# A two-layer network in float32 on one core: eight block products replaced by seven in the input, output and gate projections

## What is computed

```python
h = rmsnorm(x, norm_mix_g)
u = h @ w_in                                     # 2048 x 12288
c_g, b_g, xa, za, q, fl, iv, og, ga, gb = jnp.split(u, split_idx, axis=-1)
ya = b_g * causal_dwconv3(c_g * xa, conv_w) * silu(za)
o = hgrn2_chunked(silu(q), kk(fl), iv, log_f(fl))          # 8 heads of 128
yb = headnorm(o) * hg_norm_g * silu(og)
m = sigmoid(ga) * (ya @ w_a_out) + sigmoid(gb) * (yb @ w_b_out)
x = x + m @ w_o                                  # 2048 x 2048
gate = sigmoid(rmsnorm(x, ple_norm_g) @ w_ple_gate)        # 2048 x 2048
x = x + gate * (p @ w_ple_proj)
x = rmsnorm(x, final_norm_g)
mod = silu(c_2) @ w_ada_2 + b_ada_2              # 2048 x 6144, one row
shift, scale, gate2 = jnp.split(mod, 3)
proj = (rms_norm(x, norm_gain_2) * (1 + scale) + shift) @ w_in_2   # 2048 x 7168
out = (attention and retention of proj, gated) @ w_out_2   # 2048 x 2048
return rms_norm(x + gate2 * out, final_gain_2)
```

## Time and profile before

| | |
|---|---|
| median of 3 runs | 2703.95 us (2701.43 to 2704.10) |
| the profiled execution | 2703.86 us |
| its span in the profile | 2702.6 us |
| TensorE, busy share of the span | 98% |
| VectorE | 47% |
| ScalarE | 33% |
| GpSimd | 4% |
| mean granted clock of TensorE | 0.991 of full speed |

### The profile page before, as it was taken

The page is one execution under the profiler, slowest core; times in us unless marked ns, Lnnn a source line. Parts: engine busy times, 40 slices in busy tenths (PEclk is TensorE's granted clock), DMA queues, the critical chain, the costliest instruction groups (busy, mean ns, idle before and its releaser), DMA issues.

```text
span 2702.6 us, 28694 instructions
## 1 busy us (share of the span) xinstructions
PE 2641.6 (98%) x11724; PEld 2135.7 (79%) x11724; DVE 1267.1 (47%) x1782; ACT 879.9 (33%) x1218; POOL 98.7 (4%) x79
## 2 busy tenths in 40 slices
PE   8999999999999999999999999999999999998996
PEld 6888888888888888888888888688767777776885
DVE  7546634457334555655433444552333444442433
ACT  5533324333222222222222433332232333342331
POOL 3000000000000000000001012000000000000011
PEclk9999999999999999999999999999999999998998
DMA  5322233222334666666442222244222222221422
GB/s 179 100 79 76 76 90 101 85 71 72 90 97 141 207 206 202 202 207 206 135 161 94 86 101 86 71 146 131 75 70 78 75 81 71 78 72 53 172 94 78
DMA packets 155075, 303.86 MB, mean 112 GB/s; under 512 B 10752, under 2 KB 11008, under 8 KB 153920
## 3 DMA queue, kind: packets, MB, share of 16 engines
q1 hardware_dynamic: 154144, 300.46, 34.8%
q0 software_dynamic: 224, 1.15, 0.1%
q10 hardware_dynamic: 576, 0.43, 0.0%
HBM read 293.60 MB, written 8.39 MB: 112 GB/s over the span
## 4 chain that ended last, share of the span: by engine, by line
PE 92%; DVE 4%; issue 2%; ACT 1%; DMA 0%; POOL 0%; SPq 0%; DVEq 0%; ACTq 0%; POOLq 0%
PE bank L327 83%; PE bank L667 2%; PE bank L1099 1%; PE bank L1203 1%; PE bank L1177 1%; PE bank L383 1%; DVE WL L359 1%; PE bank L686 1%; DVE XL L452 1%; PE bank L1192 1%; PE bank L1088 1%; PE bank L324 0%; PE bank L322 0%; DMA X<-in_xT 0%; PE bank L954 0%
## 5 line engine op out<-in xcount | busy, mean ns | idle before, releaser
L327 PE MATMUL bank<-XH,WH 128*128 128x512 f32 x2816 | 1143.1, 406 | 17.3 <-DVE XL L452 10.4
L327 PE MATMUL bank<-XH,WL 128*128 128x512 f32 x2816 | 1105.8, 393 | 17.9 <-DVE WL L359 17.9
L327 PE MATMUL bank<-XL,WH 128*128 128x512 f32 x2816 | 1101.6, 391 | 0.0
L359 DVE TENSOR_TENSOR WL<-RAW,WH 128x1024 fp32r<-128x1024 f32 x436 | 538.2, 1236 | 956.5 <-ACT WH L345 955.7
L345 ACT CAST WH<-RAW 128x1024 fp32r<-128x1024 f32 x436 | 455.9, 1048 | 1209.9 <-PE bank L327 1204.5
L327 PEld LDWEIGHTS bank<-XH,WH 128*128 128x128 f32 x2816 | 533.0, 189 | 140.9 <-issue 31.4
L327 PEld LDWEIGHTS bank<-XH,WL 128*128 128x128 f32 x2816 | 531.8, 189 | 135.8 <-DVE WL L359 21.3
L327 PEld LDWEIGHTS bank<-XL,WH 128*128 128x128 f32 x2816 | 532.9, 189 | 122.9 <-issue 15.8
L327 PE MATMUL bank<-WH,XH 128*128 128x512 f32 x384 | 154.2, 401 | 0.0
L327 PE MATMUL bank<-WL,XH 128*128 128x512 f32 x384 | 149.6, 390 | 0.0
L327 PE MATMUL bank<-WH,XL 128*128 128x512 f32 x384 | 149.4, 389 | 0.0
(11 more groups left out here) (247 smaller groups left out, 1688.3 us busy)
## 6 DMA issues: line engine op xcount, KB each, us to landing
RAW<-in_w_in SPq DMA_DIRECT2D x304, 512.0 KB, 3.6
AST<-in_w_ada SPq DMA_DIRECT2D x192, 256.0 KB, 3.8
RAW<-in_w_o SPq DMA_DIRECT2D x32, 512.0 KB, 3.6
RAW<-in_w_gate SPq DMA_DIRECT2D x32, 512.0 KB, 3.6
RAW<-in_w_out SPq DMA_DIRECT2D x32, 512.0 KB, 3.6
RAW<-in_w_a SPq DMA_DIRECT2D x16, 512.0 KB, 4.1
RAW<-in_w_b SPq DMA_DIRECT2D x16, 512.0 KB, 4.3
XT<-in_xT SPq DMA_DIRECT2D x4, 1024.0 KB, 6.7
```

Of the source, the lines that this page charges most:

```text
L327: ins = nc.tensor.matmul(bank[b][:, :], l, r, start=first, stop=final)
L359: nc.vector.tensor_tensor(WL[:, m % NSPL], RAW[:, m % NRAW], WH[:, m % NSPL].bitcast(F32), ALU.subtract).then_inc(lo.sem, lo.step(m))
```

## The change

For `w_in` (all but the first 16 units), `w_o` and `w_gate`, each product of a 2x2 arrangement of blocks is made with seven products instead of eight: the 2048 features are two halves (tile k and tile k + 8), the output columns are two halves (c1 and c2), the sequence is two halves of 256 rows. The seven right-hand sides are sums of the four activation blocks, made once per operand (`sums_pool` on GpSimd, `combine_act`, `combine_dve`); the seven left-hand sides are sums of the four weight blocks, made per unit on VectorE (`weight_sums`). The seven results lie in seven halves of four banks and are added up by `seven_first` (ScalarE) and `seven_out` (VectorE). A unit is now 128 rows twice by two blocks, 256 KB, four blocks of 128 x 128; there are 872 units, of which 496 have seven products. The host lays the weights out in the order of use, and no arithmetic is done there. The other products (`raw`, `wa`, `wb`, `proj`, the second block) keep their three times four matmuls of 512 columns per unit.

The order goes by head pairs p and p + 4: `fl, q, iv, cg, xa, bg, za, og` for one pair after the other (a group is 8 units of 256 columns of output). The first 16 units make `fl` and `q` of pair 0 from the undivided x. `ga` 0 to 2 come early, the rest of `ga` and all `gb` after the pairs, `wa` and `wb` then. Branches (`y_dram`), sigmoids of the gates (`g_dram`) and `proj` (`p_dram`) go to DRAM and come back. The last third of the sum over `w_ada` moves into the second block.

```diff
+    def seven(*groups, n=8):
+        for k in range(n):
+            for name, w, c1, c2 in groups:
+                r1, r2 = 128 * k, 128 * (k + n)
+                UNITS.append((w, [(r1, c2), (r1, c1), (r2, c2), (r2, c1)]))
...
+SEVEN_PRODUCTS = ((1, 0, 1, 4), (1, 1, 4, 3), (2, 0, 3, 6), (2, 1, 6, 1), (0, 0, 2, 2), (0, 1, 5, 5), (3, 0, 0, 0))
+def split_upto(n):
+    return min(n + 2 if n else 0, len(UNITS) - 1) + 1
+def sums_upto(n):
+    return min(n + 3, len(UNITS) - 1) + 1
+def load_upto(n):
+    return min(split_upto(n) + NRAW, len(UNITS))
...
+    def pe_seven(names, ready):
...
+                for j in range(3):
...
+                    for r, half, x, wt in SEVEN_PRODUCTS:
+                        first = k == 0 and j == 0 and half == 0 and not (u and r == 3)
+                        if first and gone[u, r]:
+                            T.wait_ge(gone[u, r][0], (yield gone[u, r]))
+                        h = half or (u if r == 3 else 0)
+                        wo = (WL if j == 2 else WH)[:, s, wt]
+                        ins = nc.tensor.matmul(bank[mine[r]][:, 256 * h:256 * h + 256], wo,
+                                               (CL if j == 1 else CH)[ready][k][:, x], ...)
...
     def dve_dense(names, feed=None, ahead=2):
+            while made["sums"] < sums_upto(n):
+                    yield from weight_sums(m)
-                nc.vector.tensor_tensor(WL[:, m % NSPL], RAW[:, m % NRAW], WH[:, m % NSPL].bitcast(F32),
-                                        ALU.subtract).then_inc(lo.sem, lo.step(m))
+                nc.vector.tensor_tensor(WL[:, m % NSPL, 0:b - a], RAW[:, m % NRAW, a:b],
+                                        WH[:, m % NSPL, 0:b - a].bitcast(F32), ALU.subtract ...)
...
+    def weight_sums(m):
+        R = RAW[:, m % NRAW]
+        V.wait_ge(raw[m % NRAW], (yield raw[m % NRAW], m))
+        nc.vector.tensor_tensor(R[:, 4:6], R[:, 0:1].broadcast_to([128, 2, 128]), R[:, 1:3], ALU.subtract ...)
+        V.wait_ge(sums, (yield sums, (m, 1)))
+        nc.vector.tensor_tensor(R[:, 6], R[:, 2], R[:, 4], ALU.subtract ...)
+        V.wait_ge(sums, (yield sums, (m, 2)))
+        nc.vector.tensor_tensor(R[:, 7], R[:, 3], R[:, 6], ALU.subtract).then_inc(sums.sem, sums.step(m))
...
+    def seven_out(name):
+        V.wait_ge(ev_a, (yield ev_a, (name, "p")))
+        nc.vector.tensor_tensor(o03, two(a), o3.unsqueeze(1).broadcast_to([128, 2, 256]), ALU.add ...)
+        yield
+        nc.vector.tensor_tensor(o12, two(b), o3.unsqueeze(1).broadcast_to([128, 2, 256]), ALU.add ...)
+        nc.vector.tensor_tensor(o3, b[:, 256:512], o1, ALU.add ...)
+        nc.vector.tensor_tensor(o12, two(c), o12, ALU.add ...)
...
+    def sums_pool(tag, quarter, more, gone):
+        for j in range(8):
+            nc.gpsimd.tensor_tensor(m[:, 0:256], a[:, 256:512], a[:, 768:1024], ALU.add ...)
+            nc.gpsimd.tensor_tensor(m[:, 256:512], m[:, 0:256], a[:, 0:256], ALU.subtract ...)
+            nc.gpsimd.tensor_tensor(a[:, 256:512], a[:, 256:512], a[:, 0:256], ALU.subtract ...)
+            nc.gpsimd.tensor_tensor(m[:, 512:768], a[:, 512:768], m[:, 256:512], ALU.subtract ...)
```

More of the change, by code:

```diff
@@ L171, in _plan @@
+    seven(wide("gate", "w_gate", 0, 0), wide("gate", "w_gate", 0, 1))
+    for j in range(2, 8):
+        seven(wide("gate", "w_gate", 0, j))
+    rows = [128 * k for k in range(16)]
     qa, ka, va, zat, qr, kr, vr, zr = 0, 1024, 2048, 3072, 4096, 4608, 5120, 6144
@@ new lines, in pe_plain @@
+            kk = kmap[q] if kmap else q
+            T.wait_ge(hi, (yield hi, n))
+            T.wait_ge(xhi, (yield xhi, (ready, kk)))
+            for i in range(4):
+                c = slice(i * 128, i * 128 + 128)
+                if q == 0 and gone[i]:
+                    T.wait_ge(gone[i][0], (yield gone[i]))
+                for j in range(2):
+                    x = (xl if j else xh)(kk)
+                    if j:
+                        T.wait_ge(xlo, (yield xlo, (ready, kk)))
+                    l, r = (x[:, c], flat(WH[:, s, 0:4])) if swap else (WH[:, s, i], x)
+                    nc.tensor.matmul(bank[mine[i]][:, :], l, r, start=q == 0 and j == 0, stop=False)
@@ new lines, in pe_plain @@
+            T.wait_ge(lo, (yield lo, n))
+            for i in range(4):
+                c = slice(i * 128, i * 128 + 128)
+                l, r = (xh(kk)[:, c], flat(WL[:, s, 0:4])) if swap else (WL[:, s, i], xh(kk))
+                ins = nc.tensor.matmul(bank[mine[i]][:, :], l, r, start=False, stop=q == nk - 1)
+                done = [(name, i)] * (q == nk - 1) + [("unit", n)] * (i == 3)
+                if done:
+                    ins.then_inc(dense.sem, dense.step(*done))
+            yield from pe_turns.after_step()
@@ L328, in pe_dense @@
[L328 to L339 removed]
+                    for r, half, x, wt in SEVEN_PRODUCTS:
[5 more added lines that the diff above has]
+                        ins = nc.tensor.matmul(bank[mine[r]][:, 256 * h:256 * h + 256], wo,
+                                               (CL if j == 1 else CH)[ready][k][:, x], start=first,
+                                               stop=j == 2 and k == NK[name] - 1, skip_group_check=True)
@@ L340, in act_dense, with units_of @@
+                done = [("unit", n)] + [name] * (k == NK[name] - 1)
+                ins.then_inc(dense.sem, dense.step(*done))
+                yield from pe_turns.after_step()
+    made = {"hi": 0, "lo": 0, "load": 0, "sums": 0}
+    def units_of(names):
+        return [(k, UNIT[name, k]) for k in range(NK[names[0]]) for name in names]
+    def act_dense(names, feed=None, ahead=2):
+        for k, n in units_of(names):
+            while made["hi"] < split_upto(n):
                 m = made["hi"]
@@ L887, in build, with zero_pool @@
[L887 to L889 removed]
+    def zero_pool(p):
+        for i in range(2):
+            u = 2 * p + i
+            if u:
+                G.wait_ge(act, (yield act, ("low", u - 1, 9)))
+            nc.gpsimd.memset(RR[:, :], 0.0).then_inc(pool.sem, pool.step(("r", u)))
+            yield from idle(13)
+    y_dram = nc.dram_tensor("y_dram", [128, 8, 2, 512], F32, kind="Internal").ap()
@@ new lines, in ada_dve, with ada_column @@
+            yield
+            if k == 1 and c:
+                yield from ada_mod(c - 1)
+        yield from idle(2)
+        yield from ada_mod(7)
+    def ada_column(c, src):
+        b, was = special_bank(("ada", c), dve, ("mod", c))
+        T.wait_ge(was[0], (yield was))
+        T.wait_ge(dve, (yield dve, ("ada", 16 * c + 15)))
+        for j in range(4):
+            ins = nc.tensor.matmul(b[:, j:j + 1], src[:, 128 * j:128 * j + 128], ONES[:, 0:1], start=True, stop=True)
+            if j == 3:
+                ins.then_inc(side.sem, side.step(("ada", c)))
@@ new lines, in ada_pe, with late_ada_sp @@
+    def ada_pe():
+        yield from idle(3)
+        for c in range(8):
+            yield from idle(16)
+            yield from ada_column(c, ACC[:, c % 2])
+    def late_ada_sp():
+        Y.wait_ge(side, (yield side, ("r_1", "sum")))
+        for n in range(128, 192):
+            c, k = divmod(n, 16)
+            if n > 128:
+                Y.wait_ge(dve, (yield dve, ("ada", n - 1)))
+            nc.sync.dma_start(ASL[:, :], w_ada[k * 128:k * 128 + 128, 512 * c:512 * c + 512]
+                              ).then_inc(ld["ada0"].sem, ld["ada0"].step(n))
+            yield
+            yield
```

2163 lines of the change are left out of this document (1277 added, 886 removed).

## The result

The changed kernel takes 2950.09 us (median of 4 runs, 2939.53 to 2952.3) against 2703.43: 1.0906 times as long, 95% interval 1.0879 to 1.0933. It is slower, as forecast, but by 247 us where 124 were predicted; 2950 lies outside the range of 2750 to 2900. So the runs ask two things: where the forecast 124 us are, and where the other 122 come from.

A forecast was written before the change was run, and what follows sets the result against it. VectorE was to become the bound: eight stages sum to 1840 us, plus 13 for waits is 1853, against 1729 before, +124; added to 2703.9 this gives 2828 us. Likeliest case 2775 to 2875, wider range 2750 to 2900.

The forecast's parts named there:

- Unit prices: Seven-product units: 0.118 us per half-width matmul, 2.48 us of TensorE and 1.98 us of VectorE per unit.
- At no cost: the 872 weight loads: 256 KB weight loads: each lands in 3.8 us, issued 5 us or more before its sums, so adds nothing.
- The sign to look for: If the loads' cover is gone, VectorE waits for `raw` in front of L459.
- Stage 6: `wa` and `wb`: TensorE-bound, 64 x 2.72 + side work = 176 us.
- 1% of the 1300 us: Stages bound by VectorE: it can't be busy all the time, which adds 13 us.
- the sum: Eight stages, start to first sum of squares after `gate`, each the larger of TensorE's and VectorE's time: 1840 us.
- waits in the chains: Rival: ScalarE's extra work, SyncE's spill waits and late loads stop VectorE, 5% of 1300 us: 2890 us; chance 17%.
- Collisions: GpSimd's 32 operand sums slow VectorE at `h` by 0.55 us each, 18 us; another 18 at g.
- The clock rival: TensorE's pauses drop its clock; one unit in ten hit costs 50 x 1.7 = 85 us: 2913 us; chance 10%.
- The rest of the kernel: After `gate`: all units are plain, VectorE's work stays hidden, and this part stays as long as before.
- TensorE's gain of 120 us: The 496 seven-product units: 2.48 us of matmuls against 2.72, 0.24 us less per unit, 120 us in all.
- The first rival: TensorE stays the bound, a gain: 2704 - 120 + 56 (62 meetings) + 10 (start) = 2650 us; chance 6%.

The follow-up runs named there:

- e3: Changed kernel with SyncE's loads for the `w_ada` sum starting two steps later, so weight loads go first: 2899.03 us, ratio 1.0723.
- e9: e3 with the operand sums on VectorE instead of GpSimd, and the last gate tile stored three steps earlier: 2887.48 us, ratio 1.0684.
- e13: e3 with operand sums on VectorE, and ScalarE's cast cut to four of seven blocks from unit 61 on: 2882.38 us, ratio 1.0663.
- e14: e13 with the third weight sum of each unit made on GpSimd instead of VectorE: 2853.97 us, ratio 1.0560.
- e1: Changed kernel with one 512-column subtraction in place of the three chained weight sums (output not the reference's): 2853.84 us, ratio 1.0557.
- e2: Changed kernel with an eighth product, the seventh repeated, as more work for TensorE alone (output not the reference's): 3013.47 us, ratio 1.1148.
- e10: e3 with operand sums on VectorE, and eight unused filler matmuls before each of 12 groups, `ga` 4 to `gb` 7: 2888.22 us, ratio 1.0688.
- e4: Changed kernel without weight sums, high and low parts of 512 columns instead of 896 (output not the reference's): 2698.70 us, ratio 0.9980.
- e8: e4 with the operand sums on VectorE and the line of e5 that empties the banks moved: 2691.07 us, ratio 0.9957.
- e5: e3 with the line that empties the first 16 units' banks moved earlier; instruction order unchanged in the trace: 2898.64 us, ratio 1.0721.

## Why the prediction was right in sign and wrong in size

- **Unit prices: right.** 0.118 us per half-width matmul, 1.99 us of VectorE per unit, 0.29 us for 128 columns. The Trainium skill, "VectorE: DVE Perf Modes", section "The DRAIN you can't avoid", has the next instruction wait until the pipeline is empty, but adds that one which is not held starts earlier. The prediction weighed the first half alone; the rows agree with the second: `WL` of 1.08 us is followed 1.00 us later.
- **"At no cost: the 872 weight loads ... it is issued right after the `WL` three steps ahead of its sums": wrong, and the largest single error**, 51 of 122 us (e3). The load itself lands after 3.2 us in this stretch (2.8 in e3) and would have been hidden. Its cover was taken from the bare rule of slots, without the other orders in SyncE's queue in front of it. The sign to look for (VectorE waiting for `raw` at L459) was named, and it was there.
- **Stage 6, `wa` and `wb`: "TensorE-bound, 64 x 2.72 + side work = 176": wrong**, 204. 4 us of it are late loads (e3) and 4 the round trip through DRAM that the change adds (e9). TensorE still needs 192 us in e9, from the first matmul of `wa` to that of `wo`, where 768 matmuls fill 174. What remains is pauses for the last columns of `w_ada` and for casts; they were read in the trace and not tried.
- **"1% of the 1300 us ... adds 13": too low.** From 197 to 980 us VectorE is busy for 723 of 783, 92%; some 16 of the idle 60 us are the gaps between dependent sums that the unit price holds, the others are waits. Pairs and `ga` 1, 2 are 35 us over the sum, `wo` 6, `proj` with `gate` 5. With the late loads gone (e3), the stages in which VectorE was to be the bound are 39 us over and the start 11, 3 to 4% of the 1300 us: between the prediction's 1% and the 5% of the rival "waits in the chains". e13 and e14 show that the chain over ScalarE has a part in it. The prediction also took each stage as the larger of two times; in the pairs, where VectorE's 612 us stand beside TensorE's 549, e1 and e2 show that both count. Why `ga` 1, 2 are late was not tried.
- **Collisions: right in kind, too high in size.** 12 us at `h`, not 18. The start is 12 us late nonetheless: VectorE idles 9 of its 93 us and makes the sums of four units more than I counted.
- **The clock rival** came true in its condition and not in its price. The mean granted clock is 0.951 instead of 0.991, and 0.93 up to 1984 us, but e10, which raises it in `ga` and `gb`, wins some 3 us, not clear of the noise. In the pairs and in `gate` it was not raised, so the 85 us are refuted for one stage only.
- **The rest of the kernel** is 10 us longer, not as long as before: 19.4 us instead of 13.9 pass from the first sum of squares to the second block's first matmul, and 964 instead of 959 from there to the end. It is as long in e4, so the weight sums have no part in it; the cause stays open.
- **Two slips in the sum**, without weight: the terms of `ga` 1 and 2 add up to 44, not 45, and 5% in place of 1% of the 1300 us would give 2880, not 2890.
- **TensorE's gain of 120 us** would not have come even with VectorE free: e4 and e8 leave 5 and 12 us of it. The first rival's 2650 had 10 us for the start, where e4 loses 28 to the kernel before, and nothing for `wa`, `wb` and the rest.

## What to carry to other kernels

When work is moved from the engine that is the bound to a second one, price the second engine's whole step first: here three short sums and a subtraction, 1.99 us, filled 80% of TensorE's 2.48, and everything else then had to fit in the rest. Then walk each in-order queue, SyncE's above all, and ask what stands in front of each load: two steps of lead for an unimportant transfer cost 51 us. Where a fixed order of groups has little slack, don't take the engine's busy share to be near 100%; in such stages it was 92%. And look in the trace whether an edit changed the order at all: e5's did not.
